# Second layer's gate and up products by Strassen's seven: three of eight chunk quads per turn

## The reference

```python
def swiglu(h, w_gu, w_down):
    gu = jnp.einsum('bsd,dcf->bscf', h, w_gu)
    return jnp.einsum('bsf,fd->bsd', jax.nn.silu(gu[:, :, 0]) * gu[:, :, 1], w_down)

for l in range(DEPTH):            # DEPTH = 2
    ...
    ff = swiglu(rms_norm(h, f_pre_g[l]), f_w_gu[l], f_w_down[l])
    h = h + rms_norm(ff, f_post_g[l])
```

## Time and profile before

| | |
|---|---|
| median of 3 runs | 3001.21 us (3001.1 to 3002.56) |
| the profiled execution | 3002.15 us, its span 3000.4 us |
| PE busy | 2983.1 us, 99% of the span, 15508 matmuls |
| DVE busy | 2210.9 us, 74% |
| ACT busy | 1605.3 us, 54% |
| granted TensorE clock | 1.00 |

### The profile page before, as it was taken

How to read it: one execution, slowest core, us unless ns; L and a number is a source line. 1 busy time by engine, 2 the same in 40 slices (tenths; PEclk the granted TensorE clock), 3 DMA queues, 4 the chain that set the end, 5 groups by cost and what they waited for, 6 DMA issues and landing times.

```text
span 3000.4 us, 43910 instructions
## 1 busy us (share of the span) xinstructions
PE 2983.1 (99%) x15508; PEld 2521.3 (84%) x15508; DVE 2210.9 (74%) x2599; ACT 1605.3 (54%) x2104; POOL 61.1 (2%) x98
## 2 busy tenths in 40 slices
PE   9999999999999999999999999999999999999999
PEld 9888888888888888888888888888888788788887
DVE  6577857899989998677766665556665778888664
ACT  6655647555555555655556455555554565444543
POOL 0000000000000000000000000000000100000000
PEclk9999999999999999999999999999999999999999
DMA  9764555666665566554655666666665555676555
GB/s 335 241 192 161 188 170 170 209 196 200 199 203 194 196 198 213 191 174 148 203 169 186 220 204 203 203 211 214 204 211 196 173 184 193 224 235 212 171 191 173
DMA packets 167935, 596.91 MB, mean 199 GB/s; under 512 B 18845, under 2 KB 26201, under 8 KB 164953
## 3 DMA queue, kind: packets, MB, share of 16 engines
q1 hardware_dynamic: 150432, 545.33, 55.4%
q10 hardware_dynamic: 14888, 36.86, 3.6%
q0 software_dynamic: 2464, 12.67, 1.3%
HBM read 577.99 MB, written 17.07 MB: 198 GB/s over the span
## 4 chain that ended last, share of the span: by engine, by line
PE 87%; DVE 7%; ACT 2%; DVEq 2%; issue 1%; DMA 1%; ACTq 0%; POOLq 0%; POOL 0%; SPq 0%
PE acc L794 19%; PE acc L796 19%; PE acc L795 19%; PE tp L1302 3%; PE tp L1301 3%; PE tp L1300 3%; PE acc L800 3%; DVE lo_pair L2285 2%; PE acc L809 2%; PE acc L812 2%; PE acc L811 2%; PE acc L802 2%; PE tp L898 1%; PE acc L1300 1%; PE acc L1301 1%; PE acc L1302 1%
## 5 line engine op out<-in xcount | busy, mean ns | idle before, releaser
L2285 DVE TENSOR_TENSOR lo_pair<-raw_pair,hi_pair 128x1024 fp32r<-128x1024 f32 x1032 | 1242.2, 1214 | 536.3 <-ACT hi_pair L1540 523.7
L1540 ACT ACTIVATE hi_pair<-raw_pair 128x1024 fp32r<-128x1024 f32 x1032 | 1076.8, 1050 | 991.9 <-PE acc L796 632.5
L794 PE MATMUL acc<-hi_pair,xhl 128*128 128x512 f32 (+2 forms) x1832 | 708.6, 387 | 3.7 <-DVE xhl L2447 1.3
L796 PE MATMUL acc<-hi_pair,xhl 128*128 128x512 f32 (+2 forms) x1832 | 702.0, 383 | 0.0
L795 PE MATMUL acc<-lo_pair,xhl 128*128 128x512 f32 (+2 forms) x1832 | 701.6, 383 | 0.0
L794 PEld LDWEIGHTS acc<-hi_pair,xhl 128*128 128x128 f32 x1832 | 344.2, 188 | 73.7 <-DVE lo_pair L2285 6.0
L796 PEld LDWEIGHTS acc<-hi_pair,xhl 128*128 128x128 f32 x1832 | 344.1, 188 | 67.2
L795 PEld LDWEIGHTS acc<-lo_pair,xhl 128*128 128x128 f32 x1832 | 344.4, 188 | 64.4
L800 PE MATMUL acc<-xhl,hi_pair 128*128 128x512 f32 x640 | 229.3, 401 | 0.0
L794 PE MATMUL acc<-hi_pair,hTh 128*128 128x512 f32 x504 | 196.6, 390 | 0.0
L796 PE MATMUL acc<-hi_pair,hTl 128*128 128x512 f32 x504 | 196.1, 389 | 0.0
(11 more groups left out here) (521 smaller groups left out, 4398.9 us busy)
## 6 DMA issues: line engine op xcount, KB each, us to landing
raw_pair<-in_stream SPq DMA_DIRECT2D x1032, 512.0 KB, 4.1
turn_scratch<-made ACTq DMA_DIRECT2D x8, 1024.0 KB, 6.8
gpost<-in_post_g POOLq DMA_DIRECT2D x6, 1024.0 KB, 7.8
rotc<-turn_scratch ACTq DMA_DIRECT2D x8, 512.0 KB, 6.1
rots<-turn_scratch ACTq DMA_DIRECT2D x8, 512.0 KB, 8.3
u_stack<-u_scratch ACTq DMA_DIRECT2D x24, 128.0 KB, 4.6
h<-in_mem ACTq DMA_DIRECT2D x2, 1024.0 KB, 8.3
xT<-in_x_cols ACTq DMA_DIRECT2D x4, 512.0 KB, 6.7
```

The source lines that it names most:

```text
L794: nc.tensor.matmul(o, ah, high, start=first, stop=False)
L796: last = nc.tensor.matmul(o, al, high, start=False, stop=final)
L1540: nc.scalar.activation(hi[s][:, :, 0:w], raw[s][:, :, 0:w], ACT.Copy).then_inc(hi_done, 1)
L2285: nc.vector.tensor_tensor(lo[s][:, :, 0:w], raw[s][:, :, 0:w], hi[s][:, :, 0:w].bitcast(F32), ALU.subtract).then_inc(split_done, 1)
```

## The change

Layer 1 takes the form of layer 0, with three of the four quads of a turn in the seven products (`SEVENS = (4, 3)`) and the fourth quad plain. Its stream of weights is laid out in pairs. Layer 1 has its own `sums`, `sums_h`, `sums_l`, `x_mixed_h` and `x_mixed_l`, put where they don't meet the tables. The upper one of them lies over `gpost`, so POOL's load of that row in layer 1 waits for the end of up10. The table work of ACT and DVE stays in the turns, at other places among the splits.

```diff
-QUADS = {LG[f"gate{j}"].unit + 4 * m + k: (4 * (j - 1) + m + 1, k)
-         for j in range(1, NJ) for m in range(4) for k in range(2)}
+SEVENS = (4, 3)
+QUADS = [{LG[f"gate{j}"].unit + 4 * m + k: (n * (j - 1) + m + 1, k)
+          for j in range(1, NJ) for m in range(n) for k in range(2)} for n in SEVENS]
...
-        x_whole = at_offset("x_whole", sums_at, [P, 4, 2, T])
-        x_mixed = at_offset("x_mixed", sums_at + 8192, [P, 4, 4, P])
+        sums_at = [(free_at, free_at + 6144, free_at + 12288), (qp_at + 8192, bias_at, bias_at + 6144)]
+        mixed_at = [(free_at + 18432, free_at + 26624), (r_at + 36864, gpost_at)]
+        x_whole = at_offset("x_whole", y_at, [P, 4, 2, T])
+        x_mixed = at_offset("x_mixed", y_at + 8192, [P, 4, 4, P])
...
                     for n in range(0, 8, 2):
-                        seven(pos, j, n, o, None if n else enter)
-
-                def hidden(pos, j):
-                    product(pos, LG[f"gate{j}"], xh, xl)
-                    across(pos, j - 1)
-                    product(pos, LG[f"up{j}"], xh, xl)
-                    down(pos, j - 1)
+                        if n // 2 < SEVENS[layer]:
+                            seven(pos, j, n, o, None if n else enter)
+                        else:
+                            for i in (n, n + 1):
+                                for k in range(2):
+                                    eight(pos, j, i, o, k)
...
                 gate(pos, 0)
-                if layer < L - 1:
-                    units.before(pos, LG["up0"], 2, LU + SLOTS)
-                    act.wait_ge(mixed_made, 1)
-                    nc.scalar.activation(x_mixed_h[:, :, :, :], x_mixed[:, :, :, :], ACT.Copy).then_inc(mixed_high, 1)
+                units.before(pos, LG["up0"], 2, LU + SLOTS)
+                act.wait_ge(mixed_made, pos.n(1, 1))
+                nc.scalar.activation(x_mixed_h[layer][:, :, :, :], x_mixed[:, :, :, :], ACT.Copy).then_inc(mixed_high, 1)
                 units.ahead(pos, LG["up0"])
+                across(pos, 0)
                 if layer < L - 1:
-                    across(pos, 0)
...
                 else:
                     act.dma_start(craw[:, :, :, :].rearrange("p m s w -> p (m s w)"), c_pack).then_inc(craw_loaded, 16)
                     for j in range(1, NJ):
...
-                        gate(pos, j)
-                        across(pos, j - 1)
                         if makes:
-                            units.before(pos, LG[f"up{j}"], 3, LU + SLOTS)
+                            units.before(pos, LG[f"gate{j}"], 8, LU + SLOTS)
                             act.wait_ge(angles, c + 1)
...
-                        units.ahead(pos, LG[f"up{j}"])
-                        downs(pos, j - 1)
+                        gate_up(pos, j)
...
                     for j in range(1, NJ):
                         c = j - 2
                         g = LG[f"gate{j}"]
...
-                        units.ahead(pos, g)
-                        across(pos, j - 1)
...
-                        gate(pos, j)
-                        down(pos, j - 1)
+                        hidden(pos, j)
...
                     else:
                         pool.wait_ge(gated_c, pos.n(1, 1))
+                    if layer == L - 1 and k == 2:
+                        pool.wait_ge(unit_used, pos.n("unit", LG[f"up{NJ - 1}"].end + SLOTS))
```

More of the change, by code:

```diff
@@ L392, in build @@
         sg = gu[:, 0:NT, :]
-        hm = [at_offset(f"hm{n}", r_at + 4096 * (2 - n), [P, NT, W]) for n in range(2)]
+        hm = at_offset("hm", r_at + 8192, [P, NT, W])
         rsb = sb("rsb", [P, T])
@@ L1289, in down @@
                     for n in range(4):
-                        if n == 3 and j == NJ - 2 and layer:
-                            across(pos, NJ - 1)
-                        elif n == 2 and not layer:
+                        if n == 2:
                             across(pos, j + 1)
-                        product(pos, LG[f"down{j}_{n}"], *hidden_halves(layer, j))
+                        product(pos, LG[f"down{j}_{n}"], *hidden_halves(j))
                 def first_turn(pos, j):
@@ L1307, in seven @@
                     s, m = u % SLOTS, n // 2
-                    begin, end = n == 0, n == 6
+                    begin, end = m == 0, m == SEVENS[layer] - 1
                     near, far = slice(0, P), slice(P, 2 * P)
@@ L1311, in seven @@
                     b22, t4 = [(hi[s + 1][:, k, :], lo[s + 1][:, k, :]) for k in range(KU)]
-                    t1, t3, t2 = [(sums_h[:, k, :], sums_l[:, k, :]) for k in range(3)]
-                    mixed = [(x_mixed_h[:, k, m, :], x_mixed_l[:, k, m, :]) for k in range(4)]
+                    t1, t3, t2 = [(sums_h[layer][:, k, :], sums_l[layer][:, k, :]) for k in range(3)]
+                    mixed = [(x_mixed_h[layer][:, k, m, :], x_mixed_l[layer][:, k, m, :]) for k in range(4)]
                     pe.wait_ge(split_done, pos.n("unit", u + 1 + SLOTS))
@@ L1537, in split @@
                 if part == 1:
-                    act.wait_ge(sums_made, pos.n("quad", quad))
+                    act.wait_ge(sums_made, pos.n(f"quad{pos.layer}", quad))
                 w = width_of(pos, u)
@@ L1541, in split @@
                 if part == 1:
-                    nc.scalar.activation(sums_h[:, :, :], sums[:, :, :], ACT.Copy).then_inc(sums_high, 1)
+                    nc.scalar.activation(sums_h[pos.layer][:, :, :], sums[pos.layer][:, :, :], ACT.Copy).then_inc(sums_high, 1)
             units = Splitter(split)
@@ L2287, in split @@
                 if part == 1:
-                    dve.wait_ge(sums_high, pos.n("quad", quad))
-                    nc.vector.tensor_tensor(sums_l[:, :, :], sums[:, :, :], sums_h[:, :, :].bitcast(F32),
+                    dve.wait_ge(sums_high, pos.n(f"quad{pos.layer}", quad))
+                    l = pos.layer
+                    nc.vector.tensor_tensor(sums_l[l][:, :, :], sums[l][:, :, :], sums_h[l][:, :, :].bitcast(F32),
                                             ALU.subtract).then_inc(sums_low, 1)
@@ L2884, in down @@
                         g = LG[f"down{j}_{n}"]
-                        if n == 3 and j == NJ - 2 and layer:
-                            across(pos, NJ - 1)
-                            units.ahead(pos, g)
-                        else:
-                            units.ahead(pos, g)
+                        units.ahead(pos, g)
                         a = see_group(dve, pos, g)
@@ L2895, in down @@
                             nc.vector.tensor_tensor(part, part, a[:, :, :], ALU.add).then_inc(acc_read[g.parity], 1)
-                        if n == 1 and not layer:
+                        if n == 1:
                             across(pos, j + 1)
@@ L2963, in _, with hidden @@
+                def hidden(pos, j):
+                    gate_up(pos, j)
+                    down(pos, j - 1)
+                across(pos, 0)
+                if layer < L - 1:
                     for j in (1, 2):
@@ L3010, in _ @@
                               .then_inc(angles, 1)
-                        units.ahead(pos, g)
-                        across(pos, j - 1)
                         if j == NJ - 1:
-                            units.before(pos, LG[f"up{j}"], 4, LU + SLOTS)
+                            units.before(pos, g, 9, LU + SLOTS)
                             dve.wait_ge(b_high, 1)
```

175 lines of the change are left out of this document (76 added, 99 removed).

## The result

| | before | changed |
|---|---|---|
| median of 20 runs | 3001.39 us | 3007.47 us |
| lowest to highest | 3000.46 to 3002.65 | 3005.06 to 3010.77 |
| profiled execution, span | 3000.4 us | 3005.5 us |

The ratio is 1.0019, with a 95% interval of 1.0012 to 1.0025: 6.1 us slower, where 3006 was forecast. The 20.4 us that nine matmuls fewer a turn save are all given back. The profiled execution stands apart in one thing: its mean granted clock is 1.000, while the other 19 of the changed kernel have 0.998 or 0.999, and the 79 runs of the kernel before that stand beside the experiments all have 1.000. What the lower clock costs is seen in e11.

The account below looks back on a forecast made before the run. PE was taken to bound both layers, with DVE able to take its place. The terms -20.4 + 13.2 + 11.5 + 0.5 = +4.8 us, on the median, gave 3006 us; forecast 3003 to 3009, wider range 2994 to 3013.

Parts of the forecast that it names:

- nine matmuls fewer, ten turns: Layer 1's turns: three quads in seven products save nine matmuls, 2.04 us a turn, 20.4 us in all.
- turns 2 to 9: Layer 1, third quad: DVE's steps and ACT's activations make PE wait 1.65 us a turn, 13.2 us in eight.
- turn 1: Layer 1's first turn: DVE's wait for craw and the map operations delay PE, 11.5 us lost.
- turn 10, `b_raw`: Layer 1's last turn: b_raw's load comes as the second quad's tiles are wanted; 0 to 1.5 us, taken as 0.5.
- mixed inputs, `gpost`, `hm`: Mixed inputs beside gate0 and up0, gpost's later load, the single hm buffer: covered or free, taken as 0.
- the 0.05 "for the signal": Turns 2 to 9: 0.05 us added to each turn's wait, part of the 1.65 us a turn.
- the landing of `craw`: Turn 1: craw's load takes 7.8 us from issue to landing, so DVE waits about 4.6 us.
- the maps' 6.9: Turn 1: the map operations alone lose 6.9 us if craw lands as layer 0's DVE arrives.
- DVE didn't keep up: Rival that DVE keeps up in turns 2 to 9: 0.3 us a turn remains, 2995 us; chance 0.13.
- nothing passed on from turn to turn: Rival that waits pass on between turns: each turn loses about 2.8 us, 3015 us; chance 0.08.
- The early `craw`: Rival in turn 1: craw's load is early enough, only the maps cost, 6.9 us; 3001.4 us; chance 0.1.
- The clock rival: Turn 1: after a 5.7 us wait PE returns at half pace, 4.4 us more, 3010.4 us; chance 0.14.

Follow-up runs that it names:

- e11: The changed kernel as it is, timed and profiled once more: 3006.36 us.
- e4: Changed kernel with DVE's three steps on turn_a and ACT's sine work moved three units later, steps into the plain fourth quad: 2990.29 us.
- e5: Changed kernel with craw's load ahead of hTh, maps in the fourth quad, ACT's small activations early, DVE's steps and ACT's sine in the fourth quad: 2982.08 us.
- e1: Changed kernel with ACT's second group of four small activations ahead of the split of the second quad's first unit: 2996.18 us.
- e6: Changed kernel with two instead of three quads a turn in the seven products, nothing moved: 2996.81 us.
- e3: Changed kernel with the load of craw issued ahead of hTh instead of behind it: 3003.93 us.
- e7: Changed kernel with craw's load issued later, behind the split of the second quad's first unit: 3006.85 us.
- e2: Changed kernel with turn 1's five map operations on DVE moved into the plain fourth quad: 2997.24 us.
- e9: e5 with the fourth quad in the seven products too: 2995.48 us.
- e10: Changed kernel with craw loaded twice, the second load after the first has landed: 3011.10 us.
- e8: Changed kernel with all four quads in the seven products, table work among the down products, and craw's load ahead of hTh: 3046.72 us.

## Why the prediction held

The time was forecast at 3006, the median is 3007.47, and 3006.36 the second time. Its steps, measured in the first profile, where the clock held:

| term | forecast | measured |
|---|---|---|
| nine matmuls fewer, ten turns | -20.4 | -20.4 (turn 10 takes 64.13 us) |
| turns 2 to 9 | +13.2 | +15.2 |
| turn 1 | +11.5 | +8.5 |
| turn 10, `b_raw` | +0.5 | 0 |
| mixed inputs, `gpost`, `hm` | 0 | 0 seen |
| outside layer 1's turns | 0 | +1.8 |
| span | +4.8 | +5.1 |

**The gain** is right: the turns of e4 and e5 that lose nothing take 64.15 us on average, the 64.15 that the sum rests on.

**Turns 2 to 9** were right in mechanism and nearly in size; e1, e4 and e6 show both causes and the place. The 1.65 came out as 1.76 in turn 3: three stops cost 0.11 each where one was counted, and the 0.05 "for the signal" is shown by no row. Turns 4 (2.1) and 2 (2.5) are dearer, so the eight turns come to 15.2, 2.0 more than forecast. Turn 2 starts its second quad's sums 0.7 us later; what delays it I haven't tested.

**Turn 1** is the term that was mis-sized most, by 3.0 us, and the size that failed is the landing of `craw`: 7.8 us in the kernel before, 4.9 here. The rest of the step held. The loss is the maps' 6.9 to 7.1 plus DVE's wait for the load: 0 us of wait gave 7.1 (e3), 1.6 gave 8.5, 2.7 gave 9.7 (e7).

**The sum was closer than its parts.** 3.0 us too much in turn 1 and 0.5 in turn 10 stand against 2.0 too little in turns 2 to 9 and 1.8 that I hadn't seen. That is luck, and the 3006 deserves less trust than its distance suggests. The median moved by 6.1 us where the profiled executions differ by 5.1, so the last 1 us is not in the table at all.

**Rivals.** DVE didn't keep up, nothing passed on from turn to turn (turns 3 to 9 lose the same). The early `craw` came halfway: its price of 6.9 for the maps was right, and e3 made it whole.
The clock rival was right about the mechanism and wrong about the price. PE never stood 5.7 us in one piece, and in the first profile the clock held at 1.00. But it fell in nearly all of the changed kernel's runs, by their mean granted clock: 19 of 20 lie under 1.000, against 2 of 21 of e2 and e9, whose profiles show no fall in the turns, and none of 79 of the kernel before. Of eight profiled executions with waits of 2.08 us or more in turn 1 (changed, e11, e1, e3, e4, e6, e7, e10) it fell in seven, for 1 to 3 us of slow matmuls in excess; e9, with a wait of 2.02, kept 1.00. Most of it cost nothing: e4's turn 1 has 2.0 us of such excess and loses 8.45, the changed kernel's has none and loses 8.54. While PE waits for DVE anyway, slower matmuls only shorten the waits. It costs where PE sets the pace again: 1.2 us in e11, about 2.4 in e6, 2.8 a turn in e8. The forecast's 4.4 had assumed a whole quad, 45 matmuls, at 0.453 us; here one fall slowed at most 14, 0.43 us apart. So a fall was likelier than the 0.14 it was given, and cheaper. The four of the 20 runs with a mean clock of 0.998 took 3008.4 to 3010.6 us; they have no profile, and what the fall cost in them stays open.
The Trainium skill (TensorE: Matmul & The Clock Gate, "Why this matters for your kernels") warns of gaps in PE's work that are long enough. The trace of e6 agrees: the level fell within a wait of 3.6 us. In e7 it fell 5 us after a wait of 3.8 us had ended, and behind a second one of 2.1. In e3 it fell behind waits of 1.14 and 2.08 us that end 3.8 us apart, so on these runs shorter waits close together do it too.
